# Last layer norm of a decoder layer: its last 192 columns moved from VectorE to ScalarE and GpSimd

## What is computed

```python
def layer_norm(x, g, b):
    mu = jnp.mean(xf, axis=-1, keepdims=True)
    var = jnp.mean(jnp.square(xf - mu), axis=-1, keepdims=True)
    y = (xf - mu) * lax.rsqrt(var + LN_EPS)
    return y * g + b
...
    ffn = peer(x, peer_wq[i], peer_subkeys[i], peer_u[i], peer_v[i])
    x = layer_norm(DEEPNORM_ALPHA * x + ffn, ln2_g[i], ln2_b[i])
    gate = jax.nn.sigmoid(x @ ple_wgate[i] + ple_bgate[i])
    ple = gate * (p[i] @ ple_wproj[i])
    x = layer_norm(DEEPNORM_ALPHA * x + ple, ln3_g[i], ln3_b[i])
```

## Time and profile before

| | us |
|---|---|
| median of 3 runs | 1434.52 |
| lowest and highest run | 1433.29, 1435.02 |
| the profiled execution: its time | 1433.89 |
| its span, first to last instruction | 1431.9 |
| busy: PE, DVE, ACT, POOL | 1131.7, 1081.5, 937.0, 603.3 |

### The profile page before, as it was taken

One profiled execution on the slowest core, in us unless ns is written; L12 is line 12 of the kernel. 1 busy time (PEld: TensorE's weight loads), 2 busy tenths in 40 slices (PEclk: granted clock), 3 DMA queues, 4 the chain that ended last, 5 costly groups with the idle time before them and its releaser, 6 DMA issues.

```text
span 1431.9 us, 18884 instructions
## 1 busy us (share of the span) xinstructions
PE 1131.7 (79%) x6799; PEld 887.5 (62%) x6799; DVE 1081.5 (76%) x2603; ACT 937.0 (65%) x1611; POOL 603.3 (42%) x535
## 2 busy tenths in 40 slices
PE   9999999988779877687757977877568876876575
PEld 4567777666677666566646557766456666655454
DVE  1498777678768886778757668877888788878867
ACT  2246678679878878766646667666666766667563
POOL 1044444434353444445424434444444444445442
PEclk9999999999889989998777998888978888788879
DMA  9699999999999999999999999999999999999994
GB/s 354 254 392 424 427 426 426 429 425 425 415 425 403 425 426 427 427 426 420 426 428 426 422 426 403 424 406 411 426 427 418 425 426 427 426 426 427 427 426 146
DMA packets 90071, 586.12 MB, mean 409 GB/s; under 512 B 9741, under 2 KB 15285, under 8 KB 22522
## 3 DMA queue, kind: packets, MB, share of 16 engines
q0 software_dynamic: 74288, 536.90, 89.6%
q1 hardware_dynamic: 15690, 48.02, 8.5%
HBM read 582.79 MB, written 2.10 MB: 408 GB/s over the span
## 4 chain that ended last, share of the span: by engine, by line
DMA 40%; PE 34%; DVE 11%; ACT 8%; POOL 4%; issue 3%; POOLq 0%; DVEq 0%
DMA arena<-in_uv,ids 40%; PE ps L1164 12%; DVE arena L1770 6%; PE ps L849 5%; ACT arena L1396 4%; POOL arena L635 3%; PE ps L1059 3%; PE ps L983 3%; PE ps L669 2%; ACT actv L1389 2%; PE ps L662 2%; PE ps L679 1%; ACT gel L1386 1%; PE ps L814 1%; PE ps L746 1%
## 5 line engine op out<-in xcount | busy, mean ns | idle before, releaser
L635 POOL DMA_INDIRECT arena<-in_uv,ids x512 | 589.8, 1152 | 767.6 <-PE ps L1164 657.5
L1164 PE MATMUL ps<-ident,arena 128*128 128x128 f32 x4076 | 612.7, 309 | 279.6 <-ACT arena L1396 279.0
L1164 PEld LDWEIGHTS ps<-ident,arena 128*128 128x128 f32 x4076 | 534.9, 160 | 376.1 <-ACT arena L1396 331.4
L1770 DVE CUSTOM_DVE_ANT_1 arena<-arena 128x1024 f32<-128x1024 f32 x384 | 468.0, 1224 | 198.0 <-DMA arena<-in_uv,ids 194.5
L1396 ACT ACTIVATE arena<-arena,actv 128x1024 f32<-128x1024 f32 x511 | 554.0, 1131 | 0.0
L1386 ACT ACTIVATE gel<-hid 128x2 f32<-128x2 f32 (+1 forms) x256 | 51.9, 203 | 375.3 <-DVE hid L1770 374.5
L1770 DVE CUSTOM_DVE_ANT_0 arena<-arena 128x1024 f32<-128x1024 f32 x128 | 155.5, 1223 | 62.9 <-DMA arena<-in_uv,ids 61.9
L1389 ACT ACTIVATE actv<-gel,gates 128x1 f32<-128x1 f32 x511 | 122.8, 287 | 8.4
L849 PE MATMUL ps<-arena 128*128 128x128 f32 x992 | 127.7, 292 | 0.0
L849 PEld LDWEIGHTS ps<-arena 128*128 128x128 f32 x992 | 125.9, 209 | 0.0
L983 PE MATMUL ps<-arena 128*128 128x384 f32 x192 | 65.9, 486 | 0.0
(11 more groups left out here) (261 smaller groups left out, 996.7 us busy)
## 6 DMA issues: line engine op xcount, KB each, us to landing
arena<-in_wq SPq DMA_DIRECT2D x12, 1024.0 KB, 9.3
arena<-in_uv,ids POOLq DMA_INDIRECT x519, 12.2
arena<-in_w_out SPq DMA_DIRECT2D x2, 2048.0 KB, 11.8
arena<-in_w_gate SPq DMA_DIRECT2D x1, 4096.0 KB, 16.6
arena<-in_w_out SPq DMA_DIRECT2D x3, 1024.0 KB, 13.1
arena<-in_w_k SPq DMA_DIRECT2D x4, 512.0 KB, 7.6
arena<-in_w_q SPq DMA_DIRECT2D x2, 1024.0 KB, 10.3
arena<-in_w_v SPq DMA_DIRECT2D x2, 1024.0 KB, 10.1
```

The costliest lines, as they stand in the source:

```text
L635: nc.gpsimd.indirect_dma_start(out=rows[:, c % RING, 0:n], out_offset=None, in_=a["uv"][:, :], in_offset=bass.IndirectOffsetOnAxis(ap=ids[ ...
L1164: i = mm(ps[:, run_bank(r) + k // 4, (k % 4) * P:(k % 4 + 1) * P], rows[:, c % RING, D + k * P:D + (k + 1) * P], ident[:, :], is_transpose ...
L1770: v.tensor_tensor_reduce(out=r, in0=r, in1=x1[t], scale=1.0, scalar=0.0, op0=ALU.mult, op1=ALU.add, accum_out=hid[:, i, c:c + 1]).then_inc ...
```

## The change

`last_mean(4)` is written out at its place, with a new instruction between its two helpers that writes `negmean`, the mean times -1. VectorE centres and rescales columns 512:832 only in place of 512:1024. Columns 832:1024 are done by four instructions that wait for each other in turn: ScalarE adds `negmean` (`Identity` with a bias), GpSimd multiplies by the weights, ScalarE multiplies by `rstd` (`Copy` with a scale), GpSimd adds the bias. SyncE's third store waits for the second GpSimd instruction. Two semaphores go: `last_head` becomes one more count of `run_added`, `last_summed` is replaced by counts of `slot_free` and `y_tr`; `gate_arg` is called `tail_arg` and also counts `negmean` and `rstd`. In each of these waits the instruction waited for is the same as before.

```diff
+        negmean = sb("negmean", [P, 1])
...
             for j, (c0, c1) in enumerate(OUT_PIECES):
-                sp.wait_ge(out_ready, 2 * NT - 1 + j)
+                if j < 2:
+                    sp.wait_ge(out_ready, 2 * NT - 1 + j)
+                else:
+                    sp.wait_ge(y_pooled, 2)
                 sp.dma_start(out[0, TAILS[-1] * P:(TAILS[-1] + 1) * P, c0:c1], x2[TAILS[-1]][:, c0:c1]).then_inc(out_done, 16)
...
+            cols = slice(*OUT_PIECES[2])
+            part = x2[TAILS[-1]][:, cols]
+            pool.wait_ge(y_centred, 1)
+            nc.gpsimd.tensor_tensor(part, part, ln3_g[:, cols], ALU.mult).then_inc(y_pooled, 1)
+            pool.wait_ge(y_centred, 2)
+            nc.gpsimd.tensor_tensor(part, part, ln3_b[:, cols], ALU.add).then_inc(y_pooled, 1)
...
-                if very_last:
-                    i.then_inc(last_summed, 1)
-                else:
-                    i.then_inc(slot_free, 1)
+                i.then_inc(slot_free, 1)
...
-            pe.wait_ge(last_head, 1)
+            pe.wait_ge(run_added, NR + 1)
             gate_product(last, c0, c1, 0, 2, bank)
-            pe.wait_ge(run_added, NR + 1)
+            pe.wait_ge(run_added, NR + 2)
...
-            transposes(run_bank(NR - 1) + 1, late_sum, 0).then_inc(last_summed, 1)
+            transposes(run_bank(NR - 1) + 1, late_sum, 0).then_inc(y_tr, 1)
             first_half(2)
-            pe.wait_ge(run_added, NR + 2)
+            pe.wait_ge(run_added, NR + 3)
...
+            part = x2[TAILS[-1]][:, OUT_PIECES[2][0]:OUT_PIECES[2][1]]
+            act.wait_ge(tail_arg, 2 * (NT - 1) + 5)
+            fn(part, part, ACT.Identity, bias=negmean[:, 0:1]).then_inc(y_centred, 1)
+            act.wait_ge(y_pooled, 1)
+            act.wait_ge(tail_arg, 2 * (NT - 1) + 6)
+            fn(part, part, ACT.Copy, scale=rstd[:, 0:1]).then_inc(y_centred, 1)
...
-            def last_rstd(i):
+            def last_rstd(i, done=None):
...
-                step(v.scalar_tensor_tensor(out=rstd[:, 0:1], in0=w, scalar=1.5, in1=y, op0=ALU.add, op1=ALU.mult))
+                if done is None:
+                    step(v.scalar_tensor_tensor(out=rstd[:, 0:1], in0=w, scalar=1.5, in1=y, op0=ALU.add, op1=ALU.mult))
+                else:
+                    v.scalar_tensor_tensor(out=rstd[:, 0:1], in0=w, scalar=1.5, in1=y, op0=ALU.add, op1=ALU.mult)\
+                        .then_inc(done, 1)
+                    dve.wait_ge(done, 2 * (NT - 1) + 6)
...
-            dve.wait_ge(last_summed, 1)
+            dve.wait_ge(slot_free, NU * TOPK)
...
-            dve.wait_ge(last_summed, 2)
+            dve.wait_ge(y_tr, 2 * last + 3)
...
-            last_mean(4)
+            step(v.bn_aggr(aggr[:, :], stats[:, 0:4, :]))
+            v.tensor_scalar_add(var_e[:, 0:1], aggr[:, 1:2], EPS).then_inc(last_var, 1)
+            v.tensor_scalar(negmean[:, 0:1], aggr[:, 0:1], -1.0, None, ALU.mult).then_inc(tail_arg, 1)
+            seen.inc(v.tensor_scalar(rtmp[:, 1:2], aggr[:, 1:2], EPS, -0.5, ALU.add, ALU.mult))
             y = x2[TAILS[last]]
             centre(y[:, 0:HALF], y[:, 0:HALF], ln3_g[:, 0:HALF])
-            last_rstd(1)
+            last_rstd(1, tail_arg)
             rescale_half(y, ln3_b, 0, out_ready)
-            centre(y[:, HALF:D], y[:, HALF:D], ln3_g[:, HALF:D])
-            for c0, c1 in OUT_PIECES[1:]:
-                v.scalar_tensor_tensor(out=y[:, c0:c1], in0=y[:, c0:c1], scalar=rstd[:, 0:1], in1=ln3_b[:, c0:c1],
-                                       op0=ALU.mult, op1=ALU.add).then_inc(out_ready, 1)
+            cols = slice(*OUT_PIECES[1])
+            centre(y[:, cols], y[:, cols], ln3_g[:, cols])
+            v.scalar_tensor_tensor(out=y[:, cols], in0=y[:, cols], scalar=rstd[:, 0:1], in1=ln3_b[:, cols],
+                                   op0=ALU.mult, op1=ALU.add).then_inc(out_ready, 1)
```

More of the change, by code:

```diff
@@ L427, in build @@
         last_scaled = sem("last_scaled")
-        last_summed = sem("last_summed")
-        last_head = sem("last_head")
         slot_free = sem("slot_free")
@@ L442, in build @@
         bias_kept = sem("bias_kept")
-        gate_arg = sem("gate_arg")
+        tail_arg = sem("tail_arg")
         gain_in = sem("gain_in")
@@ L455, in build @@
         last_root = sem("last_root")
+        y_centred = sem("y_centred")
+        y_pooled = sem("y_pooled")
         out_ready = sem("out_ready")
@@ L1017, in spread_gain @@
                     pe.wait_ge(ln3_in, 16 * 2)
-                    pe.wait_ge(gate_arg, 2)
+                    pe.wait_ge(tail_arg, 2)
                 else:
@@ L1143, in background @@
                     if step == b + EMBED_1:
-                        pe.wait_ge(gate_arg, 2 * i + 1)
+                        pe.wait_ge(tail_arg, 2 * i + 1)
                         embedding_product(i, 1, 6)
@@ L1374, in gate_sigmoid @@
             def gate_sigmoid(i, n, c0, c1):
-                act.wait_ge(gate_arg, 2 * i + n + 1)
+                act.wait_ge(tail_arg, 2 * i + n + 1)
                 fn(gate[:, c0:c1], gate[:, c0:c1], ACT.Sigmoid).then_inc(gate_ready, 1)
@@ L1823, in add_head @@
                 cols = slice(0, 2 * P)
-                v.tensor_tensor(acc[NT - 1][:, cols], ps[:, bank, cols], acc[NT - 1][:, cols], ALU.add).then_inc(last_head, 1)
+                v.tensor_tensor(acc[NT - 1][:, cols], ps[:, bank, cols], acc[NT - 1][:, cols], ALU.add).then_inc(run_added, 1)
                 cols = slice(2 * P, HALF)
@@ L1869, in gate_args @@
                 v.scalar_tensor_tensor(out=gate[:, c0:c1], in0=ps[:, bank, 0:c1 - c0], scalar=rstd[:, 0:1],
-                                       in1=gate_bias[:, c0:c1], op0=ALU.mult, op1=ALU.add).then_inc(gate_arg, 1)
+                                       in1=gate_bias[:, c0:c1], op0=ALU.mult, op1=ALU.add).then_inc(tail_arg, 1)
             def y_centre(i):
```

## The result

The changed kernel takes 1440.02 us (median of 6 runs, 1438.97 to 1441.46) against 1434.77 us before (6 runs, 1433.13 to 1435.58): a ratio of 1.0035, 95% interval 1.0026 to 1.0045. It is **slower by about 5.2 us**, above the stated range. The profiled execution has a span of 1438.1 us against 1431.9.

A forecast was written before the change was run, and what follows sets the result against it. The gathers' DMA transfers were taken to set the length, with VectorE deciding the serial tail. +0.07 - 0.20 = -0.13 us gave 1433.76, or 1434.4 us as a median: no measurable change, range 1432.7 to 1436.3 us.

The forecast's parts named there:

- step 7: Merged semaphores and new waits on GpSimd, ScalarE and SyncE: nothing that mattered is queued behind them, so no cost.
- Steps 1 and 2: VectorE in the tail: added one-column instruction, +0.07 us; second centring narrowed from 512 to 320 columns, -0.20 us.
- Step 3: Last VectorE rescaling removed (0.41 us): shifts nothing itself; SyncE's queue holds the third store, which can begin 0.13 us earlier.
- Step 4: Two added ScalarE activations of 192 columns in the tail: 0.45 us each.
- Step 5: Two added GpSimd two-input instructions of 192 columns: 0.52 us each, bounds 0.35 and 1.09; start 0.07 us after ScalarE releases.
- Step 6: New ScalarE-GpSimd path ends at 1428.33, the third store can begin at 1429.49 only: hidden with 1.1 us to spare.
- the cover: What hides the new path: VectorE's work on the second piece and that piece's issue; without it, the path costs its full length.
- Rival A: Tail: two-input VectorE instructions and GpSimd's SBUF reads exclude each other; total moves from -0.13 to +0.7 us; chance 0.40.
- Rival B: GpSimd's first arithmetic after 519 gathers starts late, fetching code for 5.7 us: +4.26 us, median 1438.8; chance 0.04.
- Rival C: Gathers shift through moved addresses and longer instruction streams, either way; runs lie 1.73 us apart; chance 0.10 of deciding the difference.

The follow-up runs named there:

- e2_memset_late: The kernel before plus one GpSimd memset of an unread spare column behind the last gather, waiting for the first rescaling: 1439.46 us, ratio 1.0035 to before.
- e4_drain_first: The changed kernel plus an explicit GpSimd drain between the last gather and the two tensor instructions: 1435.73 us, ratio 1.0002 to before.

## Why the prediction was wrong

**The step that failed is step 7**, "On GpSimd the new waits stand behind the last gather ... so nothing that mattered is queued behind them". One thing was: the end of the program on that engine. I followed GpSimd's queue to its last instruction with work and took what comes after for nothing, since it was hidden. In the kernel before GpSimd is free at 1406.37 us and its closing ends at 1414.2, with 17 us to spare; the change puts its last work at 1429.72 and uses up all of it. The forecast of -0.13 us had no term for this; it is worth +4.8 us. `e2_memset_late` shows the price without the rest of the change, and `e4_drain_first` shows the change without the price. The listing of the instructions of the last line, with their start and duration, would have shown the DRAIN of 21.0 us in the trace of before.

- *Steps 1 and 2* (+0.07, -0.20) are right. Without GpSimd, variance to last issue is 4.31 us against a forecast of 4.32.
- *Step 3* holds: the third store goes behind the second, as a matter of SyncE's queue.
- *Step 4*: 0.44 and 0.46 us for 0.45. *Step 5*: 0.59 and 0.60 for 0.52, within its bounds, hop 0.08 for 0.07.
- *Step 6* is right about the store and wrong about the cover: the path ended 2.87 us after the start of the variance (1429.72 - 1426.85), forecast 2.73, and no store waited for it. As a piece of arithmetic it is hidden; as the last work of its engine it is not.
- *Rival A*, 0.40, is right in its mechanism and too large. The second centring lost 0.33 us, forecast 0.60; the one-column refinement lost nothing, it took its 0.22 us at 1428.07 with GpSimd's multiplication running until 1428.26. The collision added 0.33 us on VectorE, not 0.84. I had the multiplication wait for the end of the first centring and the addition for that of the rescaling; they started 0.11 us (1427.67, 1427.78) and 0.16 us (1429.12, 1429.28) before it. And I had counted all of the addition's duration, where VectorE was let go 0.11 us before its end.
- *Rival B*, 0.04, has the right sign and nearly the size (+4.3 us forecast, +5.2 measured), by luck. The gap before the first multiplication, which it said would show, is 0.08 us (1427.59 to 1427.67). The price lies behind GpSimd's last instruction, not ahead of its first.
- *Rival C* decides nothing: the profiled execution has its tail 1.25 us later, which is within what executions of one kernel show; the 32 runs of before in the first series lie between 1433.21 and 1438.16 us.
- *The range* left out exactly the case that happened, because GpSimd's end was bounded by the prices of rows and not by the end of the program. (A's upper bound is 1436.4 under rival A and 1436.3 in the range; nothing hangs on it.)

## What to carry to other kernels

An engine that has been idle for long at the end of a kernel is not free: look at its closing instruction, when it ends and how long after the last work, before giving it late work. After many gathers from GpSimd that closing is long, here 14 ns a gather; if GpSimd must work late, put one explicit drain directly behind the last gather, where it runs beside the other engines' work, and not within the stream. Here that gave back the loss and no more. And do not judge a tail by when its result is stored: the span ends when the last engine has closed.

## What the runs showed of the hardware

- GpSimd's closing DRAIN ends 7.8 to 7.9 us after its last work behind 519 gathers, 4.2 behind 263, 0.6 behind 7, and together with that work behind none. With 519 it was the same whatever the last work was (gather, memset of 1 or 192 columns, tensor instruction of 192 or 1024 columns).
- A VectorE instruction with two inputs in SBUF (320 columns) lost 0.33 us beside a GpSimd instruction with two inputs of 192 columns, 2.1 ns more for each column beyond, 0.09 us beside one with one input, and nothing beside a memset.
- A TENSOR_TENSOR on GpSimd took 0.59 us for 192 columns and 2.36 for 1024, so 2.1 ns a column. The first one after 519 gathers and 20 us of idleness started 0.08 us after its releaser.
